# Turning the feed-forward activations: from TensorE transposes to VectorE 32x32 blocks and ScalarE copies

## The reference

```python
D_MODEL, SEQ, DEPTH = 1024, 256, 2
D_FF = ((8 * D_MODEL // 3 + 127) // 128) * 128            # 2816

def swiglu_ffn(x, w_gu, w_down):
    a, u = jnp.split(x @ w_gu, 2, axis=-1)
    return (jax.nn.silu(a) * u) @ w_down

for l in range(DEPTH):                                    # first block
    x = layer_norm(ALPHA * x + 0.5 * swiglu_ffn(x, ffn1_w_gu[l], ffn1_w_down[l]), ...)
    x = layer_norm(ALPHA * x + hybrid_mixer(x, ...), ...)
    x = layer_norm(ALPHA * x + 0.5 * swiglu_ffn(x, ffn2_w_gu[l], ffn2_w_down[l]), ...)
for l in range(DEPTH):                                    # second block
    mod = jax.nn.silu(c) @ w_ada[l] + b_ada[l]            # shift, scale, gate of the layer
    ...
```

## Time and profile before

| what | value |
|---|---|
| median of 3 runs | 1331.56 us (1330.89 to 1331.66) |
| span of the profiled execution, first to last instruction | 1328.9 us |
| TensorE busy | 1311.6 us, 99% |
| VectorE busy | 1019.8 us, 77% |
| ScalarE busy | 675.3 us, 51% |
| mean granted TensorE clock | 0.998 of 2.4 GHz |

### The profile page before, as it was taken

The page is one execution under the profiler, slowest core; times in us unless marked ns, Lnnn a source line. Parts: engine busy times, 40 slices in busy tenths (PEclk is TensorE's granted clock), DMA queues, the critical chain, the costliest instruction groups (busy, mean ns, idle before and its releaser), DMA issues.

```text
span 1328.9 us, 18838 instructions
## 1 busy us (share of the span) xinstructions
PE 1311.6 (99%) x7096; PEld 1110.0 (84%) x7096; DVE 1019.8 (77%) x1625; ACT 675.3 (51%) x1069; POOL 105.4 (8%) x153
## 2 busy tenths in 40 slices
PE   9999999999999999999999999999999999999997
PEld 7888888788888888888887888888889998798995
DVE  6677778887777677777787887778676798966986
ACT  6444444644444344444446545444436667457672
POOL 1010100011011001111010011111000000000000
PEclk9999999999999999999999999999999999999999
DMA  8977756527767656776646358777646473463630
GB/s 268 326 232 229 226 187 208 142 96 246 244 228 233 222 185 219 223 236 228 236 161 202 102 173 292 231 253 235 221 142 200 146 237 129 143 214 118 203 128 32
DMA packets 195049, 264.92 MB, mean 199 GB/s; under 512 B 17232, under 2 KB 140240, under 8 KB 194448
## 3 DMA queue, kind: packets, MB, share of 16 engines
q1 hardware_dynamic: 183248, 223.12, 52.1%
q0 software_dynamic: 11712, 40.60, 8.9%
HBM read 262.61 MB, written 1.07 MB: 198 GB/s over the span
## 4 chain that ended last, share of the span: by engine, by line
PE 87%; DVE 7%; DMA 4%; ACT 1%; issue 1%; SPq 0%; DVEq 0%; ACTq 0%
PE ps L818 26%; PE ps L820 26%; PE ps L819 26%; PE ps L902 4%; DVE w_lo L1317 2%; DMA w_raw<-in_ffn_w_gu 2%; PE ps L1049 2%; DMA w_raw<-in_w_in 1%; PE ps L1084 1%; PE ps L1110 1%; DVE few_first L1346 1%; ACT w_hi L1141 1%; DVE y L1345 1%; PE ps L1018 0%; PE ps L1096 0%
## 5 line engine op out<-in xcount | busy, mean ns | idle before, releaser
L1317 DVE TENSOR_TENSOR w_lo<-w_raw,w_hi 128x1024 fp32r<-128x1024 f32 (+2 forms) x420 | 496.9, 1213 | 128.5 <-ACT w_hi L1141 126.5
L1141 ACT ACTIVATE w_hi<-w_raw 128x1024 fp32r<-128x1024 f32 (+2 forms) x420 | 431.0, 1053 | 247.9 <-DMA w_raw<-in_ffn_w_gu 122.0
L818 PE MATMUL ps<-w_hi,col_hi 128*128 128x512 f32 (+2 forms) x1024 | 396.7, 387 | 3.6 <-DVE w_lo L1324 1.4
L820 PE MATMUL ps<-w_hi,col_lo 128*128 128x512 f32 (+2 forms) x1024 | 392.0, 383 | 0.0
L819 PE MATMUL ps<-w_lo,col_hi 128*128 128x512 f32 (+2 forms) x1024 | 391.9, 383 | 0.0
L818 PEld LDWEIGHTS ps<-w_hi,col_hi 128*128 128x128 f32 x1024 | 192.6, 188 | 44.0 <-DVE w_lo L1317 4.3
L820 PEld LDWEIGHTS ps<-w_hi,col_lo 128*128 128x128 f32 x1024 | 192.5, 188 | 38.2
L819 PEld LDWEIGHTS ps<-w_lo,col_hi 128*128 128x128 f32 x1024 | 192.5, 188 | 34.6
L818 PE MATMUL ps<-w_hi,lat_hi 128*128 128x512 f32 (+2 forms) x544 | 208.8, 384 | 0.0
L820 PE MATMUL ps<-w_hi,lat_lo 128*128 128x512 f32 (+2 forms) x544 | 206.5, 380 | 0.0
L819 PE MATMUL ps<-w_lo,lat_hi 128*128 128x512 f32 (+2 forms) x544 | 206.3, 379 | 0.0
(11 more groups left out here) (148 smaller groups left out, 1172.8 us busy)
## 6 DMA issues: line engine op xcount, KB each, us to landing
w_raw<-in_ffn_w_gu SPq DMA_DIRECT2D x352, 256.0 KB, 4.5
w_raw<-in_w_in SPq DMA_DIRECT2D x108, 512.0 KB, 4.6
w_raw<-in_ffn_w_down SPq DMA_DIRECT2D x88, 512.0 KB, 4.9
mod<-in_w_ada POOLq DMA_DIRECT2D x32, 768.0 KB, 7.6
w_raw<-in_w_out SPq DMA_DIRECT2D x24, 512.0 KB, 4.5
norm_g<-in_ln_g POOLq DMA_DIRECT2D x8, 512.0 KB, 4.2
norm_b<-in_ln_b POOLq DMA_DIRECT2D x8, 512.0 KB, 6.1
w_raw<-in_w_out SPq DMA_DIRECT2D x16, 256.0 KB, 4.5
```

Source lines behind the costliest of these rows:

```text
L818: pe.matmul(dst, a_hi, b_hi, start=start, stop=False)
L820: return pe.matmul(dst, a_lo, b_hi, start=False, stop=stop)
L1141: act.activation(half_of(w_hi[j], n, h), half_of(raw[j], n, h), ACT.Copy).then_inc(hi_ready, 1)
L1317: tt(half_of(w_lo[j], n, h), half_of(raw[j], n, h), half_of(w_hi[j], n, h).bitcast(F32), ALU.subtract)\
```

## The change

In all rounds of a feed-forward stage but the last, the job `ht` is replaced by three jobs.

- `hturn`: one VectorE instruction transposes every 32x32 block of `hidden` (128 partitions by 512 columns) within its group of 32 partitions.
- `hmove`: sixteen ScalarE copies of 32 partitions by 128 columns bring each block to the group of partitions where it belongs. The first of them waits for `hturn`.
- `hparts`: the split into `lat_hi` (ScalarE, two copies of 128x256) and `lat_lo` (VectorE, two subtractions of 128x256), now from SBUF.

The last round of a stage keeps `ht`. The four TensorE transposes are gone in 40 of the 44 rounds. The products, the weights' splits and the side work are the same instructions as before.

```diff
@@ def ffn_jobs(s): (the rounds from 2 on)
     for r in range(2, ROUNDS):
-        jobs += gu(r, 0) + [("ht", s, r - 1)]
+        if r == 2:
+            jobs += gu(r, 0)[:1] + moved(1) + gu(r, 0)[1:]
+        else:
+            jobs += gu(r, 0)
+        jobs += parts(r - 1)
...
         jobs += gu(r, 1)
+        if r < ROUNDS - 1:
+            jobs += blocks(r)
         if lag < ROUNDS - TAIL:
-            jobs += down(lag, 0) + down(lag, 1)
+            jobs += down(lag, 0) + moved(r) + down(lag, 1)
             lag += 1
+        elif r < ROUNDS - 1:
+            jobs += moved(r)
         if r < 2 + MOD_STEPS:
             jobs += [("modsplit", s, r - 2)]
@@ TensorE
                 elif kind == "down":
                     r, i = job[2:]
-                    turns_done(("ht", s, r))
+                    if r < ROUNDS - 1:
+                        pe.wait_ge(h_split, at["hparts", (s, r)])
+                    else:
+                        turns_done(("ht", s, r))
@@ ScalarE
+                elif kind == "hmove":
+                    r = job[2]
+                    act.wait_ge(h_turned, at["hturn", (s, r)])
+                    if at["hturn", (s, r)] > 1:
+                        act.wait_ge(h_split, at["hturn", (s, r)] - 1)
+                    for b in range(4):
+                        for a in range(4):
+                            act.activation(h_cols[32 * b:32 * b + 32, a, :], h_blocks[32 * a:32 * a + 32, b, :], ACT.Copy)\
+                                .then_inc(h_moved, 1)
+                elif kind == "hparts":
+                    r = job[2]
+                    q = 2 * (r % 4)
+                    act.wait_ge(h_moved, at["hmove", (s, r)])
+                    if r >= 4:
+                        act.wait_ge(used, NUMBER[s, ("down", r - 4)] + 1)
+                    act.activation(h_part(lat_hi, q)[:, 0], h_as_columns[:, 0], ACT.Copy)
+                    act.activation(h_part(lat_hi, q)[:, 1], h_as_columns[:, 1], ACT.Copy).then_inc(hi_part, 1)
@@ VectorE
                     if r >= 2:
-                        b, n = TURN["ht", s, r - 2][0]
-                        dve.wait_ge(turned[b], n + 1)
+                        dve.wait_ge(h_turned, at["hturn", (s, r - 2)])
...
+                elif kind == "hturn":
+                    r = job[2]
+                    dve.wait_ge(hidden_done, at["hidden", (s, r, 1)])
+                    if at["hturn", (s, r)] > 1:
+                        dve.wait_ge(h_moved, 16 * (at["hturn", (s, r)] - 1))
+                    dve.transpose(h_blocks.rearrange("p b (c t) -> p b c t", t=32),
+                                  hidden[:, r % 2, :, :].rearrange("p i (g b f) -> p b (i g) f", g=2, b=4)).then_inc(h_turned, 1)
+                elif kind == "hparts":
+                    q = 2 * (job[2] % 4)
+                    dve.wait_ge(hi_part, at["hi_part", job])
+                    tt(h_part(lat_lo, q)[:, 0], h_as_columns[:, 0], h_part(lat_hi, q)[:, 0].bitcast(F32), ALU.subtract)
+                    tt(h_part(lat_lo, q)[:, 1], h_as_columns[:, 1], h_part(lat_hi, q)[:, 1].bitcast(F32), ALU.subtract)\
+                        .then_inc(h_split, 1)
```

More of the change, by code:

```diff
@@ L165, in ffn_jobs @@
     down = lambda r, i: [("down", s, r, i)]
+    blocks, moved, parts = (lambda r, kind=kind: [(kind, s, r)] for kind in ("hturn", "hmove", "hparts"))
     if s == 0:
@@ L169, in ffn_jobs @@
         jobs += gu(0, 1)[:1] + first((6, 7)) + [("xt", s, 1, 1)] + gu(0, 0)[1:] + gu(0, 1)[1:]
-        jobs += gu(1, 0)[:1] + [("ht", s, 0)] + gu(1, 0)[1:] + [("params", s)] + gu(1, 1)
+        jobs += blocks(0) + gu(1, 0)[:1] + moved(0) + gu(1, 0)[1:] + parts(0) + [("params", s)] + gu(1, 1) + blocks(1)
     else:
         jobs = gu(0, 0)[:1] + halves(s, ("gu", 1, 1)) + gu(0, 0)[1:] + gu(1, 0)[:1] + xt(s, 1) + halves(s, ("gu", 2, 0))
-        jobs += gu(1, 0)[1:] + gu(0, 1) + [("params", s)]
-        jobs += gu(1, 1)[:1] + [("ht", s, 0)] + gu(1, 1)[1:]
+        jobs += gu(1, 0)[1:] + gu(0, 1) + blocks(0) + [("params", s)]
+        jobs += gu(1, 1)[:1] + moved(0) + gu(1, 1)[1:] + blocks(1) + parts(0)
     lag = 0
     for r in range(2, ROUNDS):
-        jobs += gu(r, 0) + [("ht", s, r - 1)]
+        if r == 2:
[3 more added lines that the diff above has]
+        jobs += parts(r - 1)
         if r > 2:
@@ L453, in count_jobs @@
                     ENDS["sums", s, tile] = ENDS[group]
-        if kind in ("xt", "ht", "trlat", "ycols"):
+        if kind in ("xt", "ht", "hparts", "trlat", "ycols"):
             COUNT.add("hi_part", job)
+        if kind in ("hturn", "hparts"):
+            COUNT.add(kind, job[1:])
+        if kind == "hmove":
+            COUNT.add(kind, job[1:], 16)
         if kind == "ycols" and not TURN[job]:
@@ L640, in build @@
         hidden = arena[:, 512:1536].rearrange("p (r t n) -> p r t n", r=2, t=TT)
+        h_blocks = arena[:, 1536:2048].rearrange("p (b n) -> p b n", b=4)
+        h_cols = arena[:, 2048:2560].rearrange("p (a n) -> p a n", a=4)
         rows1 = arena[:, 0:TT * IN1].rearrange("p (t n) -> p t n", t=TT)
@@ L710, in build @@
          weighed, y_cols, ret_mixed, half_sum, var_ready, rstd_ready, h_ready, x_ready, y_ready, rope_done, rotated, idx_w_ready,
-         idx_summed, rope_a_done, rope_k_done, squares, latent, folded, mod_summed, mod_hi, mod_lo, mod_row) = (
+         idx_summed, rope_a_done, rope_k_done, squares, latent, folded, mod_summed, mod_hi, mod_lo, mod_row,
+         h_turned, h_moved, h_split) = (
             sem(n) for n in ("group_done", "silu_done", "hidden_done", "copied", "hi_part", "scores", "score_free", "maxed",
@@ L714, in build @@
                              "h_ready", "x_ready", "y_ready", "rope_done", "rotated", "idx_w_ready", "idx_summed",
-                             "rope_a_done", "rope_k_done", "squares", "latent", "folded", "mod_summed", "mod_hi", "mod_lo", "mod_row"))
+                             "rope_a_done", "rope_k_done", "squares", "latent", "folded", "mod_summed", "mod_hi", "mod_lo", "mod_row",
+                             "hidden_blocks_turned", "hidden_blocks_moved", "hidden_split"))
         x_in = [[sem(f"x_landed{i}{h}") for h in range(2)] for i in range(TT)]
@@ L747, in sink_of, with h_part @@
             return sinks.rearrange("p (f j) -> p f j", f=2)[:, :, pairs[0]:pairs[-1] + 1]
+        def h_part(tile, q):
+            return tile[:, q:q + 2, :].rearrange("p g (i a t) -> p g i a t", i=TT, a=4)
+        h_as_columns = h_cols.rearrange("p a (i g t) -> p g i a t", i=TT, g=2)
         def sum_banks(s, i):
```

## The result

The changed kernel takes 1478.45 us (median of 4 runs, 1477.53 to 1480.21), the kernel before 1331.22 (4 runs): a ratio of 1.1108, 95% interval 1.1092 to 1.1124. It is slower, as forecast, but by 147 us and not by 49; 1478 lies outside 1350 to 1420.

The account below looks back on a forecast made before the run. TensorE, with work in 99% of the span, was taken as the bound. Waits of 62.8 us less 14.4 of transposes brought the span from 1328.9 to 1377.3, the median to 1380 us; range 1350 to 1420, 8 times in 10.

Parts of the forecast that it names:

- The path: TensorE loses four transposes in 40 rounds, 14.4 us; `spread` then waits for `modsplit` behind the copies, 62.8 us in all.
- The loop with the prediction's own step: VectorE's queue plus standstill, with copies 0.20 us apart: 17.86 us a round; 15.1 from round 9 to 10.
- T: End of the first tile's `gu` on TensorE, from which one round was timed; 72.20 us in round 4 of stage 0.
- the copies' price: Sixteen `hmove` copies on ScalarE at a step of 0.20 us, 3.2 us a round; bounds 0.10 and 0.28.
- no overlap: Upper bound for the step of the ScalarE copies, 0.28 us each.
- the rival with dearer links: Copies that don't overlap (0.28) and `hturn` at 1.23 us add 59 us, giving 1439; chance 0.10.
- The factor of 32: Each microsecond in the chain of copies and `hturn` moves eight waits in four stages, so 32 us in all.
- the wait of round 10: TensorE's wait at the `spread` of round 10, put at 3.9 us in each of four stages.
- The waits at the first `spread` of the four stages: TensorE's waits at `spread` of round 3: 2.1 us in stage 0, 4.9 in stages 2, 3 and 5.
- The block transpose: `hturn`, 128x512 on VectorE, put at 0.69 us with bounds of 0.43 and 1.23.
- The rival with the clock: The clock falls to its lower level for the `gu` after seven long waits: 34 us more, 1414; chance 0.12.
- The rival in which the cover holds: With a copy step of 0.12 us or less, waits of rounds 4 to 9 vanish, giving 1329 us; chance 0.12.

Follow-up runs that it names:

- e1: Changed kernel with only one of the sixteen copies made per round after the program's first round, values not those wanted: 1316.91 us, ratio 0.9893.
- e3: Changed kernel with the sixteen copies on all 128 partitions, without the move between partition groups, values not those wanted: 1393.09 us, ratio 1.0465.
- e6: Changed kernel with `modsplit` put behind the second tile's `gu`, ahead of the block transpose: 1453.51 us, ratio 1.0921.
- e10: Changed kernel with ten 128x128 matmuls of ones, result unread, ahead of each `spread`: 1475.72 us, ratio 1.1087.
- e4: Changed kernel reordered: a round's copies behind the next round's first `gu`, ahead of `spread`, their split behind the second `gu`: 1326.49 us, ratio 0.9965.
- e8: Order of e4 with `modsplit` ahead of the block transpose, earlier first copies in stages behind the first, one copy increment a round: 1322.40 us, ratio 0.9936.
- e12: Changed kernel with all copies, from the program's second round, 32 partitions from first to second group, values not those wanted: 1401.45 us, ratio 1.0524.
- e5: Changed kernel with copies of 32 partitions inside their own groups in even rounds, 64 partitions in odd rounds, values not those wanted: 1414.49 us.
- e9: Changed kernel with the copies' two loops exchanged, source group outermost, every copy made: 1478.34 us, ratio 1.1106.

## Why the prediction was right in direction and wrong in size

- *The path.* Right: TensorE's 14.4 us come off (e1), and `spread` behind `modsplit`, behind the low halves, behind the copies, is where the time goes, 32 times. The loop with the prediction's own step gives its own numbers (e3: 17.85, 14.88). One sum on the way is off: the two low halves behind `modsplit` end at T + 18.8 by its own terms, not T + 18.5. The forecast does not use it.
- *The failed step: the copies' price.* "I take 0.20 ... and 0.28 (no overlap)". Measured 0.333. Two things were off. That neighbours overlap was read from pairs that span all 128 partitions, and so begin at the same one; the sixteen copies do not. And the bound "no overlap" was laid at 0.28 where a copy by itself takes 0.31 and 0.02 follow. The second bound was thus too low, and the rival with dearer links, which had the mechanism, got only 0.10. VectorE's round is 16 x 0.133 = 2.1 us longer than forecast: the 19.98 less 17.86.
- *The factor of 32.* Each microsecond in the chain was taken to count eight times a stage. The step alone is worth 1475.7 - 1389.0 = 86.7 us of span (the changed kernel less e3), and 86.7 / 2.13 is 41. By the starts of the `spread`s 59.2 of it lie from round 3 to round 10 of the four stages, which is 28 times 2.13, as counted; 25.2 lie ahead of the first `spread`s, which is 12 times and not four (the other 2 lie behind round 10 and at the program's end). In the first rounds three `hmove` stand one behind the other ahead of the first `spread`, and the prediction's rule counted one. That all three count fits these numbers, and that they count through the link to `spread` fits e6, where some 6 us a stage went with it; no run varied their number.
- *The rest, 12 us (e3's span of 1389.0 less the forecast's 1377.3).* Three things were sized too low or passed over, 13 us together; the wait of round 10, a little shorter than forecast, takes 1 back. The waits at the first `spread` of the four stages are 5.57, 4.37, 5.16 and 6.12 in e3, 21.2 in all, where 2.1 and three times 4.9 were taken, 16.8. The lower clock behind round 10 costs 5 us there (see below). And a job that the working passed over, `fold` in the last of these stages, puts three instructions of 1.22 us between `modsplit` and the low halves on VectorE; the round there is 21.4 in e3 and not 17.85, and 23.5 in the changed kernel and not 19.98. In VectorE's timeline of the changed kernel:

```profile
1032.81 1.22 DVE L1529 SCALAR_TENSOR_TENSOR att<-arena,norm_b 128x1024 f32<-128x1024 f32 x1
1034.06 1.22 DVE L1530 TENSOR_TENSOR arena<-arena,att 128x1024 f32<-128x1024 f32 x1
1035.20 1.22 DVE L1531 SCALAR_TENSOR_TENSOR arena<-arena,norm_g 128x1024 f32<-128x1024 f32 x1
```

- *The block transpose.* 0.69 taken, 711 ns measured (40 times). Right, and so are `hparts` and the high half behind the copies (1.09 for 1.11).
- *The rival with the clock.* The clock fell, and by that rival it would cost 34 us. In the rounds from 3 to 9 it costs nothing that the runs show (e10): the matmuls at 1.2 GHz run where TensorE would have waited for VectorE anyway, at the first `spread`s too, where the rival put 12 us. Behind the `spread` of round 10 it is lost in full, as the rival said, since no wait follows there: 7.19, 7.14, 7.26 and 7.99 us in the four stages for 5.71 before, 6.8 us in all. The rival took 22, the whole `gu` at the lower level; in stage 0 the step is 0.43 us for the first seven of its 24 matmuls and 0.23 to 0.26 from then on.
- *The rival in which the cover holds* fell. It does hold in another order (e4, e8).

## What to carry to other kernels

A price read off neighbours that overlap holds only for neighbours of the same kind: ask of an added instruction also where its partitions start, and lay the outer bound above the full duration of one. In a round that two engines share, a wait is worth its length times the number of its links in a chain, start of the stage included; follow the first rounds by themselves. And a slow step need not be made faster if it can stand beside work that the waiting engine has anyway: the order gave 152 us, where the forecast's step would have given 85 (e3).

## What the hardware showed

On ScalarE a copy whose first partition, read or written, differs from that of the copy before began only 0.02 us after that one's end: copies of 128 columns follow each other at 0.333 us then and at 0.201 otherwise, with 128 partitions (e3) as with 32 that cross groups (e12); 64 and 32 inside their groups add up to the same two steps (e5). It is enough that the read side changes (twelve steps of fifteen in the changed kernel) or the written side (e9). The Trainium skill ("VectorE: DVE Perf Modes", Two Vector instructions with no wait between them) states such a rule for VectorE: an instruction whose start quadrant (group of 32 partitions) differs, on the side read or on the side written, from that of the last one to read or write the same memory is held until the earlier ones have finished. These runs agree with it on ScalarE for SBUF; on VectorE no run here varies it. For the copies that do overlap, the Trainium skill ("ScalarE: Activation LUTs", What ACT_TABLE_LOAD costs) gives 186 ns + 0.833 ns an element, which makes an estimate of 293 for 128, and an overlap of 93: measured 295 and 94 (e3). The copies whose first partition changes have no such overlap.
